# Front phase of a diffusion step: order of the weights' rests, of two fetches and of one doubled piece

## The reference

```python
mod = silu(c) @ w_ada + b_ada              # six rows of 2048: sh1, sc1, gate1, sh2, sc2, gate2
h = rms(x, g_attn) * (1 + sc1) + sh1
q_a, kv_c, k_r, gu, gv, ga, gb = split(h @ w_in)   # widths 512, 256, 64, 2048 x 4
q = rms(q_a, g_qa) @ w_qb
ckv = rms(kv_c, g_kv)                      # the key and value latents
v = rms(gelu(gv), g_sgu)                   # each group of 256 channels mixed by w_s
o_b = gelu(gu) * (w_s @ v + b_s)
```

## Time and profile before

| what | value |
|---|---|
| median of three runs | 3488.33 us |
| profiled execution, its own time | 3489.2 us |
| its span, first to last instruction | 3487.4 us |
| TensorE busy | 3289.7 us, 94% |
| VectorE, ScalarE, GpSimd busy | 2107.1, 1409.7, 365.9 us |
| mean granted TensorE clock | 0.972 |
| weights' rests, front (L588) | 72 instructions, 161.7 us |

### The profile page before, as it was taken

How to read it: one execution, slowest core, us unless ns; L and a number is a source line. 1 busy time by engine, 2 the same in 40 slices (tenths; PEclk the granted TensorE clock), 3 DMA queues, 4 the chain that set the end, 5 groups by cost and what they waited for, 6 DMA issues and landing times. The chain is left out here.

```text
span 3487.4 us, 39961 instructions
## 1 busy us (share of the span) xinstructions
PE 3289.7 (94%) x16088; PEld 2553.8 (73%) x16088; DVE 2107.1 (60%) x1830; ACT 1409.7 (40%) x1295; POOL 365.9 (10%) x429
## 2 busy tenths in 40 slices
PE   6889999999999899998999999939999999999995
PEld 4678878888788799987888888725666666666663
DVE  3336545455552677763233242257898898888886
ACT  3122212221111344442121221236777777777774
POOL 0020010010000000000011111030111111111102
PEclk9999999999999999999999999969999999999997
DMA  9465545465553101125353454358999999999996
GB/s 381 183 167 201 187 158 197 158 235 195 186 190 133 39 33 46 36 85 197 110 186 133 148 168 143 106 206 331 376 392 384 392 398 378 388 400 392 385 406 230
DMA packets 142462, 790.13 MB, mean 227 GB/s; under 512 B 18992, under 2 KB 30288, under 8 KB 61408
## 3 DMA queue, kind: packets, MB, share of 16 engines
q1 hardware_dynamic: 101680, 668.72, 50.0%
q0 software_dynamic: 40656, 119.60, 11.2%
HBM read 720.39 MB, written 67.86 MB: 226 GB/s over the span
## 5 line engine op out<-in xcount | busy, mean ns | idle before, releaser
L102 DVE TENSOR_TENSOR w_lo<-w_stage,w_hi 128x2048 fp32r<-128x2048 f32 x384 | 881.5, 2300 | 140.6 <-ACT w_hi L97 140.6
L97 ACT ACTIVATE w_hi<-w_stage 128x2048 fp32r<-128x2048 f32 x384 | 736.9, 1920 | 307.4 <-PE e_ps L109 307.4
L107 PE MATMUL i_ps<-w_hi,hT_hi 128*128 128x512 f32 (+1 forms) x1440 | 569.0, 395 | 31.1 <-DVE w_lo L588 13.4
L108 PE MATMUL i_ps<-w_lo,hT_hi 128*128 128x512 f32 (+1 forms) x1440 | 559.2, 388 | 0.0
L109 PE MATMUL i_ps<-w_hi,hT_lo 128*128 128x512 f32 (+1 forms) x1440 | 559.2, 388 | 0.0
L107 PE MATMUL e_ps<-w_hi,xgT_hi 128*80 128x512 f32 x1024 | 404.1, 395 | 2.5 <-DVE xgT_lo L2080 2.3
L108 PE MATMUL e_ps<-w_lo,xgT_hi 128*80 128x512 f32 x1024 | 403.9, 394 | 0.0
L109 PE MATMUL e_ps<-w_hi,xgT_lo 128*80 128x512 f32 x1024 | 401.4, 392 | 0.0
L107 PE MATMUL p_ps<-w_hi,xT_hi 128*128 128x512 f32 x960 | 378.3, 394 | 6.8 <-DVE xT_lo L1575 6.8
L109 PE MATMUL p_ps<-w_hi,xT_lo 128*128 128x512 f32 x960 | 374.7, 390 | 0.0
L108 PE MATMUL p_ps<-w_lo,xT_hi 128*128 128x512 f32 x960 | 374.4, 390 | 0.0
(11 more groups left out here) (322 smaller groups left out, 4436.3 us busy)
## 6 DMA issues: line engine op xcount, KB each, us to landing
w_stage<-in_w_e SPq DMA_DIRECT2D x384, 1024.0 KB, 8.6
w_stage<-in_w_ada SPq DMA_DIRECT2D x96, 1024.0 KB, 6.7
w_raw<-in_w_in SPq DMA_DIRECT2D x64, 1024.0 KB, 4.9
w_stage<-in_w_o_gm SPq DMA_DIRECT2D x16, 1024.0 KB, 6.8
w_stage<-in_w_o_mla SPq DMA_DIRECT2D x16, 1024.0 KB, 5.2
w_stage<-in_w_out SPq DMA_DIRECT2D x16, 1024.0 KB, 4.8
acts<-evacuated POOLq DMA_DIRECT2D x60, 256.0 KB, 3.9
side<-acts POOLq DMA_DIRECT2D x40, 256.0 KB, 5.7
```

The lines of the kernel that those rows point to most:

```text
L97: act.activation(dst, src, ACT.Copy).then_inc(st.hi, 1)
L102: dve.tensor_tensor(dst, src, hi.bitcast(F32), ALU.subtract).then_inc(st.split, 1)
L107: pe.matmul(out, x_hi, w_hi, start=first, stop=False)
L108: pe.matmul(out, x_hi, w_lo, start=False, stop=False)
```

## The change

In the order of the diff: the second accumulation that stood at piece 55 now stands at piece 43, so that accumulations 34 to 47 stand one piece earlier. The stores of the q tiles go to an array of five blocks [128, 512], a tile each, 2 KB to a partition in one run; they are read back by ten transfers of 256 KB, which write four runs of 512 B in a partition, and the two reads of krT come before them instead of after. `mod_store(0)` moves behind `gv_load(0)` in GpSimd's list. On VectorE `dense_lo(g)` moves ahead of `columns(g)` and `modulate(g)`. TensorE waits for hT_lo k tile by k tile.

```diff
--- before.py
+++ after.py
@@ -222,7 +222,7 @@
     W_CHUNK = {c: c - 2 + 4 if c < GU else c - 6 if c < GA else c - 2 for c in range(2, N_CH)}
     BLOCKS = 4
     ADA2_AT = [n for n in range(2 * KG, KG * N_CH - KG) if n not in (2 * KG + 1, 2 * KG + 3)]
-    ADA2_AT = sorted(ADA2_AT + [n for n in range(11 * KG, KG * N_CH) if n % KG == 3][:BLOCKS * KT - len(ADA2_AT)])
+    ADA2_AT = sorted(ADA2_AT + [n for n in range(10 * KG, KG * N_CH) if n % KG == 3 and n != 55][:BLOCKS * KT - len(ADA2_AT)])
     assert len(ADA2_AT) == BLOCKS * KT
 
     with ExitStack() as ctx:
@@ -376,8 +376,7 @@
             for t in range(TT):
                 pool.wait_ge(q_lo, t + 1)
                 for h in range(2):
-                    pool.dma_start((M.qaT_lo_d if h else M.qaT_hi_d)[:, :, bass.ts(t, P)],
-                                   stg[t % 2][h][:].rearrange("p (j n) -> p j n", j=KG)).then_inc(q_out[t % 2], 16)
+                    pool.dma_start((M.qaT_lo_d if h else M.qaT_hi_d)[t], stg[t % 2][h][:]).then_inc(q_out[t % 2], 16)
             pool.wait_ge(k_hat, 1)
             pool.dma_start(O["new_ckv"][0, 0], ev[:, 0, 0:KV_LORA]).then_inc(ctx_out, 16)
             pool.wait_ge(rot, 2)
@@ -393,13 +392,13 @@
                     pool.dma_start(M.ckvT_d[:, :, bass.ts(t, P)], stg_f[t % 2][:].rearrange("p (j n) -> p j n", j=2)).then_inc(kv_out[t % 2], 16)
             for c in range(GV, GU):
                 chunk_store(c)
-            mod_store(0)
             for b in range(2):
                 pool.wait_ge(kv_out[b], 16 * (11 - 3 * b))
             pool.wait_ge(ctx_out, 48)
             pool.dma_start(wsT[:].rearrange("p g n -> p (g n)"), I["w_sT"]).then_inc(consts2, 16)
             pool.dma_start(b_col[:], I["b_sT"]).then_inc(consts2, 16)
             gv_load(0)
+            mod_store(0)
             for i in range(4):
                 if i < 3:
                     gv_load(i + 1)
@@ -411,8 +410,11 @@
                 pool.wait_ge(g_out[t], 16 * 4)
             for b in range(2):
                 pool.wait_ge(q_out[b], 32 * (3 - b))
-            for dst, src in ((M.qaT_hi, M.qaT_hi_d), (M.qaT_lo, M.qaT_lo_d), (M.krT_hi, M.kvT_hi_d[:, 2, :]), (M.krT_lo, M.kvT_lo_d[:, 2, :])):
+            for dst, src in ((M.krT_hi, M.kvT_hi_d[:, 2, :]), (M.krT_lo, M.kvT_lo_d[:, 2, :])):
                 pool.dma_start(dst[:], src).then_inc(back_in, 16)
+            for dst, src in ((M.qaT_hi, M.qaT_hi_d), (M.qaT_lo, M.qaT_lo_d)):
+                for t in range(TT):
+                    pool.dma_start(dst[:, :, bass.ts(t, P)], src[t].rearrange("p (j n) -> p j n", j=KG)).then_inc(back_in, 16)
             for c in range(GA, N_CH):
                 if c == N_CH - 1:
                     mod_store(3)
@@ -423,7 +425,7 @@
                 chunk_store(c)
                 if c == 13:
                     mod_store(2)
-            pool.wait_ge(back_in, 64)
+            pool.wait_ge(back_in, 16 * (2 + 2 * TT))
 
         @block.scalar
         def _(act):
@@ -702,9 +704,9 @@
             dve.wait_ge(ev_act, 2 * TT)
             dve.wait_ge(ev_dve, 2 * TT)
             for g in range(KG):
+                dense_lo(g)
                 columns(g)
                 modulate(g)
-                dense_lo(g)
                 modulated(g)
             for n in range(KG, KG * N_CH):
                 dense_lo(n)
@@ -768,12 +770,12 @@
                 n, w = KG * c + g, WIDTH[c]
                 if t == 0:
                     pe.wait_ge(d_split, n + 1)
-                    if c == 0:
-                        pe.wait_ge(h_lo, KG * g + KG)
                 if g == 0 and c:
                     pe.wait_ge(acc_free, TT * (c - 1) + t + 1)
                 for j in range(KG):
                     k = KG * g + j
+                    if c == 0 and t == 0:
+                        pe.wait_ge(h_lo, k + 1)
                     ins = product(pe, ps[t][:, 0:w], M.hT_hi[:, k, bass.ts(t, P)], M.hT_lo[:, k, bass.ts(t, P)],
                                   W.hi[:, n % 2, bass.ts(j, w)], W.lo[:, n % 2, bass.ts(j, w)], k == 0, k == KT - 1)
                 if t == TT - 1:
@@ -2410,7 +2412,7 @@
     M.h2 = dram("h2", [N_TOK, D])
     M.obT = dram("obT", [D, N_TOK])
     rounded = lambda name, shape: nc.dram_tensor(name, shape, F32R, kind="Internal").ap()
-    M.qaT_hi_d, M.qaT_lo_d = (rounded(f"qaT_{h}_d", [P, KG, N_TOK]) for h in ("hi", "lo"))
+    M.qaT_hi_d, M.qaT_lo_d = (rounded(f"qaT_{h}_d", [TT, P, KG * P]) for h in ("hi", "lo"))
     M.kvT_hi_d, M.kvT_lo_d = (rounded(f"kvT_{h}_d", [P, 3, N_KEY]) for h in ("hi", "lo"))
     M.ckvT_d = dram("ckvT_d", [P, 2, N_TOK])
     todo = [lambda: phase_front(nc, M, I, W, O),
```

## The result

The changed kernel takes 3459.26 us, the median of four runs between 3456.75 and 3460.88. The kernel before took 3488.38 us on the same chip (four runs, 3486.27 to 3488.47). The ratio is 0.9918, with a 95% interval from 0.9905 to 0.9930: faster by 29.1 us.

The account below looks back on a forecast made before the run. TensorE paces the front, so its stalls and the half clock after them are the gain: 14.5 + 3.0 + 10.7 + 7.4 = 35.6 us, from 3489.2 to 3453.6, or 3452.7 for a median; range 3446 to 3461.

Parts of the forecast that it names:

- the doubled piece: Stall near 911 us: the row sum a piece earlier removes 4.9 us of wait and 2.5 of clock, 7.4 us.
- The early part: Three hT_lo stalls at 83.5, 113.0 and 139.1 us: rests ahead of modulation, waited tile by tile, save 14.5 us.
- The fourth group's term: Stall at 139.13 us: 4.4 of its 6.19 us go, plus 2.5 us of clock, 6.9 us.
- The third group's 3.8: Stall at 112.98 us, 3.42 us long: same pattern as the one at 83.54, so 3.8 us again.
- The second group's 3.8: Stall at 83.54 us: 3.3 us of stall plus 1.6 of clock, less 1.1 of new w_ada wait, 3.8 us net.
- rival (2): Small matmuls are DMA-bound and the clock still falls at the three early stalls: 6.6 us there, 3460.6 us; chance 0.10.
- The query inputs: Two rounds of q stores before chunk 1's evacuation, stall at 202.6 us: 2 KB runs land sooner, saving 3.0 us.
- their landing in 2.3 to 4 us: Sign expected in the changed profile: the q stores land in 2.3 to 4 us.
- Rival (3): The q stores' layout makes no difference, since other traffic held them: 3455.7 us; chance 0.10.
- The gate rows: Stall near 477 us: slice fetched ahead of the modulation rows' stores, removing 8.0 us of wait and 2.7 of clock, 10.7 us.
- The clock's terms: Slow matmuls after the stalls near 477 and 911 us: 2.7 and 2.5 us counted as regained.
- Rival (1): Reads from 718 us delay piece 44's load beyond 19.7 us: slower, chance 0.03, or the gain eaten, 0.02.

Follow-up runs that it names:

- A: The changed kernel with all parts of the change, against the kernel before: 3459.26 us, ratio 0.9918.
- second profile of A: The changed kernel run again unaltered, against the kernel before: 3457.10 us, ratio 0.9914, 30.9 us faster.
- Experiments 7 and 8: 7: changed kernel, TensorE waiting for the whole group's hT_lo again, 3463.79 us; 8: changed kernel, raw pieces 1 to 3 behind their group's last w_ada piece, 3453.12 us.
- the held kernels: Changed kernel, with new and with old query store layout, each with SP's two 1 MB loads held until the fifth q tile is split: 3453.99 and 3455.77 us.
- kernels 5 and 6: 5: kernel before with only the second accumulation moved to piece 43, 3481.44 us; 6: kernel before with only gate rows' fetch ahead of modulation rows' stores, 3478.63 us.
- kernel 4: Kernel before with only rests ahead of the modulation and TensorE's hT_lo wait k tile by k tile: 3474.57 us, ratio 0.9963.

## Why the prediction was right, and where its sum was not

The forecast was 3452.7 us, in a range from 3446 to 3461; 3459.3 came. It is faster by far more than 0.2%, by the mechanisms that were named, but the sum of 35.6 us is 6.5 above the 29.1 of this comparison (4.7 above the 30.9 of the second).

**The stalls.** Right in place and kind. The waits at 476.98 and 911.03 are gone, `gv_norm(0)` waits for nothing, and the doubled piece's sum comes a piece earlier. Of the three hT_lo waits two are gone, and 1.76 us are left of the third (1.7 was foreseen).

**The early part, 14.5 predicted, 12.7 measured.** The fourth group's term, 6.9, measured 6.93. The third group's 3.8 measured 4.4. Its wait for w_ada was 0.95 us where 1.1 was booked, and the clock gave back more than the 1.6: 10 slow matmuls follow the stall at 112.98 in the kernel before (2.1 us), 7 the one at 83.54 (1.5 us). The second group's 3.8 measured 2.5, and 1.0 in the second profile of A. The step that failed is the new wait for w_ada. I had the piece land at 84.1, by adding 2.5 us at 421 GB/s to the raw piece's landing, and be wanted at 83.0, 1.1 us. It was 2.34 us, where the longest wait for w_ada had been 1.8. The piece was wanted when I said (84.34 in a group that started 1.24 us later), but the interval behind the raw piece is 3.9 us and not 2.5. The kernel before shows that already: its piece was issued at 75.67 and took 9.7 us, so it landed at 85.4. The landing was there to be read, and I computed it. In one of the two profiles of A the wait brought the low clock with it. (The three steps add up to 13.8 in the profiles; the medians of the part alone give 12.7, with 8 to 17 as the interval, so that the two don't differ.)

Experiments 7 and 8 tell what makes the wait. With the raw piece behind it in the queue it is gone. With the raw piece still ahead, but the instruction packet an interval later, the piece is there in time as well. So the wait of A comes with both; the first is shown by an edit, the second isn't. The lower bound of this part, rival (2), is refuted as a whole (6.6 was its sum), though its mechanism is what is left at this one place.

**The query inputs, 3.0 predicted, 0.6 measured.** This is the largest miss. I worked it out from the landing times of quiet stores, 3.6 and 2.3 us, and carried them to a first round that had taken 5.5 us, while the same rows said that something else held that round. Beside SP's two loads the new stores take 5.8 us in the first round, and their landing in 2.3 to 4 us, which was to be a sign, failed there. Only in the second, 2.7 in place of 3.4, does the layout show. Rival (3) had this right, at a tenth of the chance: it gave 3455.7. The row for it, "the first round took 5.5 and not 3.6 us", stood in my text and should have halved the term.

What the traces say of the layout itself is another matter. With the loads held, equal bytes take 2.7 us from issue to split in runs of 2 KB and 3.3 in runs of 512 B. The rule of the Trainium skill ("DMA: Bandwidth & Descriptors", Specifications), line rate from 512 B on, foresaw no gain, and comes near to what the change brought; but that is the traffic's doing, and the held kernels don't bear the rule out. They differ by 0.6 us in this round, about half of it issue time on GpSimd and about half landing, and by 1.4 us over the step. The traffic in A covers most of that. The same page says under "Queues, rings and completion order" that each DMA engine takes turns between the queues that have work for it, a packet at a time. The trace agrees in that stores of GpSimd's queue went from 2.7 to 5.8 us beside SP's loads; turns by the packet no run here shows.

**The gate rows, 10.7 predicted, 9.3 measured; the doubled piece, 7.4 predicted, 6.5 measured.** By the profiles they are 10.9 and 7.1, so the stalls and their ends were read rightly. The clock's terms, 2.7 and 2.5 us, were taken from one execution that showed 13 and 12 slow matmuls; kernels 5 and 6 show 8 and 7 at the same places, 1.7 and 1.5 us, and kernel 4 agrees with them by its steps. A term counted off one trace was booked as if every execution paid it.

**What was costed at nothing.** The ten reads, in the DMA issues of A from 690 to 712 us (KB each, us to landing):

```profile
w_raw<-in_w_in SPq DMA_DIRECT2D x3, 1024.0 KB, 8.9
qaT_hi<-qaT_hi_d POOLq DMA_DIRECT2D x5, 256.0 KB, 19.3
qaT_lo<-qaT_lo_d POOLq DMA_DIRECT2D x5, 256.0 KB, 22.6
```

They land after 19 and 23 us, where the slowest transfer there took 19.2 before. SP's three input pieces beside them land in 8.9 us by the median; piece 44's own load, issued at 693.50, takes 8.9, and the longest of the three 10.7. Rival (1) decides at 19.7. So it is refuted here, with 11 us to spare. My reason against it, that SP's queue is another one, was a poor one: the q stores show that one queue's traffic does delay the other's. Here the delay was small: the same piece's load took 9.3 us before the change.

**Beside the sum** lie +1.24 us at the start and +0.5 behind the heads. The early one is no effect of the change: the second group starts at 75.35 and 74.75 us in the kernels with the doubled piece and the gate rows alone, which are the same up to there, and at 74.14 in A again.

So of the 6.5 us that were too many, 2.4 are the query stores, 1.8 the early part (by its median), 1.4 and 0.9 the two late places: 6.5. Each of the last three is uncertain by more than its size; the first is the surest, as nine profiles show it.

**The range held with some luck.** Its lower side is added wrongly: 1.5, 2.2, 1 and 1 make 5.7 and not 6.5. Its upper side, 3461, rests on rival (2)'s 6.6, and that is lower than its own terms: without the clock the first two groups give 3.3 - 1.1 = 2.2 each, with the third's 4.4 that is 8.8, and the rival's time would be 3458.4. The measured 3459.3 lies above that.

Left open: the wait of 3.37 us for chunk 1's evacuation, at 189.36 us in A, and the half clock behind it are in all of these kernels (3.4 to 4.6 us). What the instruction packet costs was not tested either. An edit that takes the wait away was not tried.

## What to carry to other kernels

A stall at an engine that paces everything is worth its own length plus what the clock takes behind it, but the second part differs from execution to execution: count it from several profiles, or give it as a range. When a wait is taken away, look at the queue of what is wanted next, and move what nobody wants yet behind it; here that one line was worth 3.3 us by the steps. Where a trace has the landing of the transfer that will be waited for next, read it and don't work it out from a bandwidth. Before a transfer is made faster by its shape, see what else is in flight when it leaves: three microseconds of the wait were two loads that could have left later.

## What was not expected of the hardware

The same stall of 4.88 us was followed by 12 matmuls at half speed in one execution (2.5 us) and by 7 in another (1.5 us). The same wait of 2.34 us was followed by none in one (small matmuls 1.07 us) and by the low clock in another (1.93 us).

Two 1 MB loads in SP's queue that leave 3 us ahead stretch a round of 256 KB stores in GpSimd's queue from 2.7 to 5.8 us, five times the 0.6 us that the length of the runs makes in a quiet DMA, issue time included. Issuing is dearer with shorter runs too: two stores in a row took 0.73 and 0.85 us of GpSimd's queue in runs of 512 B and 0.55 and 0.56 in runs of 2 KB.

In each of the twelve profiles one interval between the landings of SP's 1 MB pieces, between 81 and 92 us, is 3.7 to 4.0 us long where most are 2.5, and a 16 KB packet of the instruction queue falls into it.

Phases with the same code took from 2339.8 to 2346.0 us in twelve profiles, a spread twice as large as some of the gains that were looked for.
